# Attention pipelines of a two-block transformer: another step order, probabilities turned a step later, negated minima, and clock fillers

## The chip, the cores and the metric

The kernel runs on one core of a Trainium2 chip. The metric is the device time of one execution in microseconds, median of the runs. One execution was also recorded by the hardware profiler; its rows are what this document reads.

## The reference

Two transformer blocks over 256 tokens of width 1024, in float32. The first block has two layers. Each projects the normed input to twelve groups of columns and runs four attentions with four heads each on them:

```python
a_out = neighbourhood_attention(na_q, na_k, na_v, rel_bias)      # scores + bias, softmax
a = softmax(s1 + alibi) - lam * softmax(s2 + alibi)              # differential attention
b_out = rms_norm(a @ df_v, diff_subln) * (1.0 - lambda_init)
c_out = gqa_attention(rope(rms(gq_q)), rope(rms(gq_k)), gq_v)    # 4 heads, 2 key/value heads
d_out = mla_attention(q_nope, q_rope, k_nope, k_rope, mla_v)
x = x + rms_norm(concat(a_out, b_out, c_out, d_out) @ w_o)       # then a gated FFN
```

`lam` is exp(sum(q1*k1)) - exp(sum(q2*k2)) + lambda_init. The second block has four layers with an FFN each: nsa (compressed, selected and window attention, here 16 causal softmax units of one head), stick-breaking attention, a gated depthwise convolution with layer norm, and moba (8 causal softmax units).

## The kernel before

Five engines run programs of their own, ordered by semaphores that are written out by hand. Weights come in 1 MB pieces into four slots; ScalarE makes a rounded copy `w_hi`, VectorE the rest `w_lo`, and TensorE does three products for each pair (`three`, L2008 to L2010). Activations are split likewise into `hT_hi` and `hT_lo`.

**First block's mixer.** `add_gemm(... (4, 3, 0, 1, 2))` projects the columns in chunks of 512, chunk 4 first, each into two PSUM banks of `acc`, evacuated by ScalarE (token tile 0) and VectorE (tile 1). Between chunks run the latent projections, the rotations (on GpSimd, `gq_rotate` and `ml_rotate`) and the bias flips. In the middle of the last chunk, `jobs_early` turns eight groups of projected tiles (na, gq, mla) into `tiles`. Then `mix_A` runs 20 steps, each two heads (or the two softmaxes of one differential head) of one tile of 128 queries, in `STEP_ORDER`: indices 0 to 3 are neighbourhood steps, 4 to 11 differential, 12 to 15 grouped, 16 to 19 latent. The order is N N N N D D G D D G D D G D D G M M M M.

In turn i of its loop TensorE issues the scores of step i (L2302), turns the probabilities of step i-2 (L2315, into `tr`) and multiplies those of step i-3 with the values (L2335, or L2329 for differential steps). VectorE in turn i takes the negated, scaled minima of step i (L1708 with a bias, L1704 without) and scales the probabilities of step i-1 (L1725, L1726; L1720 to L1722 for differential ones). ScalarE in turn i does the two exponentials of step i (L1254) and the copy of `tr` for step i-2 to `probT` (L1264). Scores lie in two pairs of banks by turns. The differential queries and keys are turned after the scores of step 1 (`diff_jobs`), since their columns come with the last chunk. The exponential for lambda opens ScalarE's `mix_A`. After the last differential step VectorE's `diff_norm` copies the outputs out of `acc`, squares, sums and takes the root in one go, `diff_gain` follows two turns later, and TensorE turns the result at turn 21 (`diff_turn`). Outputs go to `hT_hi` (ScalarE) and `hT_lo` (VectorE) by `pair_out_hi` and `pair_out_lo`. In `pair_steps`, both grouped heads of a step write the same half of the output partitions, and their four products run head after head (`apart` False); in the other steps they alternate between the heads.

**Second block's units.** `unit_pipeline` does the same for nsa and moba, with one head and both query tiles a unit: VectorE adds the bias and takes maxima (L1573), and one more instruction makes `nmx` of them (L1580) before ScalarE's exponentials (L1207). Probabilities are turned (L2242) two units behind the scores (L2227) and multiplied (L2266) three behind, after ScalarE's copy (L1215).

`keep_clock(bank, count)` (L2039) issues products of a constant that nobody reads. Before, it stands only in front of four norms, nine products each.

Of the kernel before, what the change touches and what calls it, by code (L numbers as in the profile page):

```python
# [55 lines left out]
STEP_ORDER = (0, 1, 2, 3, 4, 5, 12, 6, 7, 13, 8, 9, 14, 10, 11, 15, 16, 17, 18, 19)  # L56
NA_LAST, DF_LAST, GQ_LAST = (max(STEP_ORDER.index(i) for i in range(a, b)) for a, b in ((0, 4), (4, 12), (12, 16)))
GQ_FIRST, ML_FIRST = (min(STEP_ORDER.index(i) for i in range(a, a + 4)) for a in (12, 16))
GQ_STEPS = range(12, 16)
JOBS_EARLY, JOBS_A = 8, 10  # L60
EARLY = 4
QUAD = 32
# [145 lines left out]
def make_plan(A):  # L208
# [15 lines left out]
    for index, (kind, l) in enumerate(LAYERS):  # L224
        if kind == "A":
# [3 lines left out]
            def up_projections():  # L229
# [4 lines left out]
            g1 = add_gemm(plan, A["w_in"][l], D, A_IN, "proj", (4, 3, 0, 1, 2), {2: up_projections})  # L234
# [5 lines left out]
                      "lam_ready": 1, "lam_exp": 1, "hT_tr": 1, "kcat_a": 2, "od_ready": 1, "od_taken": 1})  # L240
# [4 lines left out]
            g2.order = (0, 1, 4, 5, 2, 3, 6, 7)  # L245
# [136 lines left out]
def first_second_block(nc, A, out, conv_rows, where_both, where_first, where_second):  # L382
    plan, phases = make_plan(A)
    with ExitStack() as ctx:
# [166 lines left out]
        O_PLACE = {0: 0, 1: 1, 2: 4, 3: 5, 4: 0, 5: 1, 6: 2, 7: 3}  # L551
# [9 lines left out]
        def pair_steps():  # L561
# [3 lines left out]
            def pair(heads, bias=None, scale=1.0, diff=None):  # L565
                for qt in range(TT):
                    steps.append(dict(qt=qt, heads=heads, bias=bias and [b[:, S * qt:S * qt + S] for b in bias],
                                      scale=scale, diff=diff, apart=True))
# [19 lines left out]
            for i in range(GQ_STEPS.start, GQ_STEPS.stop):  # L588
                steps[i]["apart"] = False
# [121 lines left out]
        def jobs_for(kind):  # L711
# [3 lines left out]
            if kind == "A":  # L715
                one = [proj[:, t, col("gq_k"):col("gq_k") + P] for t in range(TT)]
                ks = [[kcat[:, t, 2 * j + i, :] for i in range(2) for t in range(TT)] for j in range(2)]
                return [(two(col("na_q")), tiles[:, 0:2, :], 1.0), (two(col("na_k")), tiles[:, 2:4, :], 1.0),
# [4 lines left out]
                        (two(col("df_q")), tiles[:, 4:6, :], 1.0), (two(col("df_k")), tiles[:, 6:8, :], 1.0)]  # L723
# [114 lines left out]
        def _(pool):  # L838
# [9 lines left out]
            def gq_rotate(ph):  # L848

                pool.wait_ge(sem["gq_root"], n["gq_root"] + 1)  # L850
                for t in range(TT):
# [16 lines left out]
                    def perm(v):  # L868
                        return v[:, 0:4, :].rearrange("p (b a) c -> p a b c", a=2)
                    dst = gq[t][:, 0:4, :].rearrange("p (a b) c -> p a b c", a=2)  # L870
                    link(nc.gpsimd.tensor_tensor(dst, perm(t1), perm(t2), ALU.add))
# [106 lines left out]
        def _(act):  # L978
# [45 lines left out]
            def gemm(ph):  # L1024
                for i, (n0, w, pieces) in enumerate(ph.chunks):
# [12 lines left out]
                    if ph.mix is not None and ph.mix.kind == "mixA" and i == 4:  # L1038
                        for j in range(JOBS_EARLY):
                            _, dst, scale = jobs_for("A")[j]  # L1040
                            evac_job(j, dst, scale, n["pt_ready"])
# [130 lines left out]
            def A_3(ph):  # L1172
                act.wait_ge(sem["lat_a"], n["lat_a"] + 2)
                act.wait_ge(sem["lat_d"], n["lat_d"] + 2)
                for t in range(TT):
                    kv = proj[:, t, A_IN:A_IN + W].rearrange("p (h c) -> p h c", h=ML_H)
                    nc.scalar.activation(kcat[:, t, :, 0:HD], kv[:, :, 0:HD], ACT.Copy).then_inc(sem["kcat_a"], 1)

# [16 lines left out]
            def unit_pipeline(us, jobs, extra={}):  # L1195

                with_T = [i for i, u in enumerate(us) if u["pair"] != 0]
                for i in range(len(us) + 3):
                    if i < len(us):
# [3 lines left out]
                        for qt in range(TT):  # L1203
                            c, cols = 2 * slot + qt, score_columns(u, qt)
                            dst = scores_of(slot)[:, cols]
                            src = dst if u["bias"] is not None else up[:, i % 2, cols]
                            nc.scalar.activation(dst, src, ACT.Exp, bias=nmx[:, c:c + 1],  # L1207
                                                 scale=u["scale"], accum_out=den[:, c:c + 1]).then_inc(sem["p_exp"], 1)
                    if i >= 2 and (i - 2) in with_T:
                        j = with_T.index(i - 2)  # L1210
# [3 lines left out]
                        width = S + P if us[i - 2]["causal"] else TT * S  # L1214
# [9 lines left out]

            def mix_A(ph):
                act.wait_ge(sem["lam_ready"], n["lam_ready"] + 1)
                nc.scalar.activation(lam[:, 0:2], lam[:, 2:4], ACT.Exp).then_inc(sem["lam_exp"], 1)

                def diff_turned():

                    for j in range(JOBS_EARLY, JOBS_A):
                        _, dst, scale = jobs_for("A")[j]
                        if j > JOBS_EARLY:
                            evac_job(j, dst, scale, n["pt_ready"])
                            continue
                        act.wait_ge(sem["pt_ready"], n["pt_ready"] + j + 1)
                        for a in range(2):
                            ins = nc.scalar.activation(dst[:, a, :], tr[:, j % 2, S * a:S * a + S], ACT.Copy,
                                                       scale=c1("df_scale")[:, a:a + 1])
                        ins.then_inc(sem["pt_evac"], 1)  # L1240

# [5 lines left out]
                for i in range(len(steps) + 3):  # L1247
                    if i < len(steps):
                        step, slot = steps[i], i % 4
                        act.wait_ge(sem["s_max"], n["s_max"] + i + 1)  # L1250
                        for u in range(2):
                            c, dst = 2 * slot + u, prob[:, slot, u, :]
                            src = dst if step["bias"] is not None else pair_bank(i, u)
                            nc.scalar.activation(dst, src, ACT.Exp, bias=nmx[:, c:c + 1], scale=-1.0,  # L1254
                                                 accum_out=den[:, c:c + 1]).then_inc(sem["p_exp"], 1)
# [1307 lines left out]
```

## Time and profile before

| | us |
|---|---|
| median of 3 runs | 1963.43 (1956.75 to 1965.12) |
| profiled execution | 1959.28 |
| its span, first to last instruction | 1957.5 |
| TensorE busy | 1867.2 (95%) |
| VectorE busy | 1138.0 (58%) |
| ScalarE busy | 921.6 (47%) |
| GpSimd busy | 175.0 (9%) |
| mean granted TensorE clock | 0.981 |

Busy time of TensorE has modelled ends, so pauses are read from the starts of its instructions, and from the idle time that a row gives in brackets with what ended it. The granted clock of a stretch is 1.00 at 2.4 GHz and 0.50 at 1.2 GHz. L numbers are lines of the kernel above. In the timeline, neighbouring instructions of one kind are merged, with their count behind the x.

### The profile page before, as it was taken

How to read it: one execution, taken by the hardware profiler on the slowest of the kernel's cores; microseconds unless marked ns; L12 is line 12 of the kernel's file. 1: busy time of each engine (PE TensorE's matmuls, PEld its weight loads, DVE VectorE, ACT ScalarE, POOL GpSimd, SP SyncE). 2: the span in 40 equal slices, each digit the busy share in tenths (PEclk: the TensorE clock that was granted, in tenths of full speed). 3: DMA queues.
4: the chain of work that ended last, by engine and by line, in shares of the span. 5: the costliest groups of instructions: out<-in, count | busy, mean ns of one | idle time of the engine just before them, and what ended most of it. 6: DMA issues, size and time to landing. Idle time of an engine off the chain costs nothing. (4 is left out here: it accounts for less than half of the span.)

```text
span 1957.5 us, 29109 instructions
## 1 busy us (share of the span) xinstructions
PE 1867.2 (95%) x11568; PEld 1634.4 (83%) x11568; DVE 1138.0 (58%) x1647; ACT 921.6 (47%) x1267; POOL 175.0 (9%) x213
## 2 busy tenths in 40 slices
PE   7899999988999999899999999999889999989998
PEld 6668999766899978689998789998669998769997
DVE  6676555757655578554446465446765546765443
ACT  4564334456434446554435355345245435564342
POOL 1300000040000030001000001002501002000000
PEclk9999999999999999799999999999989999989999
DMA  7504555550355555126555425554725554524551
GB/s 249 181 22 147 175 183 185 181 172 12 129 193 193 191 187 180 49 87 215 176 204 177 172 86 175 201 182 169 219 90 172 173 202 147 203 91 173 181 204 66
DMA packets 185356, 313.08 MB, mean 160 GB/s; under 512 B 18877, under 2 KB 67571, under 8 KB 185267
## 3 DMA queue, kind: packets, MB, share of 16 engines
q1 hardware_dynamic: 182595, 304.24, 46.0%
q0 software_dynamic: 1376, 4.38, 0.9%
q10 hardware_dynamic: 1296, 3.24, 0.5%
q8 instruction: 60, 0.98, 0.2%
q14 instruction: 29, 0.24, 0.0%
HBM read 309.90 MB, written 1.94 MB: 159 GB/s over the span
## 5 line engine op out<-in xcount | busy, mean ns | idle before, releaser
L1459 DVE TENSOR_TENSOR w_lo<-raw,w_hi 128x2048 fp32r<-128x2048 f32 (+2 forms) x290 | 654.0, 2285 | 289.7 <-ACT w_hi L995 289.0
L995 ACT ACTIVATE w_hi<-raw 128x2048 fp32r<-128x2048 f32 (+2 forms) x290 | 533.5, 1877 | 107.5 <-PE tr L2010 59.8
L2008 PE MATMUL acc<-w_hi,hT_hi 128*128 128x512 f32 (+2 forms) x688 | 270.1, 393 | 13.3 <-DVE w_lo L1459 7.3
L2010 PE MATMUL acc<-w_hi,hT_lo 128*128 128x512 f32 (+2 forms) x688 | 266.4, 387 | 0.0
L2009 PE MATMUL acc<-w_lo,hT_hi 128*128 128x512 f32 (+2 forms) x688 | 266.3, 387 | 0.0
L2008 PE MATMUL acc<-w_hi,aux_hi 128*128 128x512 f32 x608 | 237.2, 390 | 0.0
L2009 PE MATMUL acc<-w_lo,aux_hi 128*128 128x512 f32 x608 | 237.2, 390 | 0.0
L2010 PE MATMUL acc<-w_hi,aux_lo 128*128 128x512 f32 x608 | 236.6, 389 | 0.0
L2008 PE MATMUL up<-hT_hi,w_hi 128*128 128x256 f32 x768 | 217.8, 284 | 0.6 <-DVE w_lo L1459 0.6
L2009 PE MATMUL tr<-hT_lo,w_hi 128*128 128x256 f32 x768 | 217.5, 283 | 0.0
L2008 PE MATMUL tr<-hT_hi,w_hi 128*128 128x256 f32 x768 | 217.5, 283 | 0.0
L2010 PE MATMUL tr<-hT_hi,w_lo 128*128 128x256 f32 x768 | 217.5, 283 | 0.0
L2010 PE MATMUL up<-hT_hi,w_lo 128*128 128x256 f32 x768 | 217.4, 283 | 0.0
L2009 PE MATMUL up<-hT_lo,w_hi 128*128 128x256 f32 x768 | 217.4, 283 | 0.0
L2008 PEld LDWEIGHTS acc<-w_hi,hT_hi 128*128 128x128 f32 x688 | 130.5, 190 | 41.8 <-issue 8.9
L970 POOL TENSOR_TENSOR proj<-proj 128x512 f32<-128x512 f32 x64 | 66.3, 1056 | 1010.9 <-ACT proj L1388 1010.9
L2010 PEld LDWEIGHTS acc<-w_hi,hT_lo 128*128 128x128 f32 x688 | 130.7, 190 | 25.6
L2009 PEld LDWEIGHTS acc<-w_lo,hT_hi 128*128 128x128 f32 x688 | 130.8, 190 | 24.6 <-issue 0.5
L2008 PEld LDWEIGHTS up<-hT_hi,w_hi 128*128 128x128 f32 x768 | 147.3, 192 | 2.7 <-DVE w_lo L1459 1.0
L2009 PEld LDWEIGHTS up<-hT_lo,w_hi 128*128 128x128 f32 x768 | 147.3, 192 | 1.7
L2009 PEld LDWEIGHTS tr<-hT_lo,w_hi 128*128 128x128 f32 x768 | 147.5, 192 | 0.0
L2008 PEld LDWEIGHTS tr<-hT_hi,w_hi 128*128 128x128 f32 x768 | 147.5, 192 | 0.0
(361 smaller groups left out, 2761.1 us busy)
## 6 DMA issues: line engine op xcount, KB each, us to landing
raw<-in_mlp_w_up SPq DMA_DIRECT2D x64, 1024.0 KB, 6.6
raw<-in_mlp_w_down SPq DMA_DIRECT2D x64, 1024.0 KB, 5.4
raw<-in_ffn_w_gate_up SPq DMA_DIRECT2D x88, 512.0 KB, 4.8
raw<-in_ffn_w_down SPq DMA_DIRECT2D x22, 1024.0 KB, 5.1
raw<-in_w_in SPq DMA_DIRECT2D x16, 1024.0 KB, 8.2
raw<-in_sb_w_in SPq DMA_DIRECT2D x12, 1024.0 KB, 5.3
raw<-in_moba_w_in SPq DMA_DIRECT2D x12, 1024.0 KB, 5.3
raw<-in_nsa_w_in SPq DMA_DIRECT2D x10, 1024.0 KB, 6.3
```

Source lines behind the costliest of these rows:

```text
L970: nc.gpsimd.tensor_tensor(ffn_r2[:, W * j:W * j + W], r, r, ALU.mult)\
L995: nc.scalar.activation(w_hi[:, p0.slot, 0:p0.floats], raw[:, p0.slot, 0:p0.floats], ACT.Copy)\
L1459: nc.vector.tensor_tensor(w_lo[:, p0.slot, 0:m], raw[:, p0.slot, 0:m], f32(w_hi[:, p0.slot, 0:m]), ALU.subtract).then_inc(sem["lo_ready"], 1)
L2008: nc.tensor.matmul(dst, hi, whi, start=first, stop=False)
L2009: nc.tensor.matmul(dst, hi, wlo, start=False, stop=False)
L2010: return nc.tensor.matmul(dst, lo, whi, start=False, stop=last)
```

## The change

- The step order becomes D G D G D D G D D G D D N N N N M M M M. The chunks of w_in are taken as 4, 3, 2, 1, 0, so that the neighbourhood's queries and keys come last; `jobs_early` turns the differential tiles (with their two scales) instead, and the na tiles follow after step 4's turn (`late_jobs`).
- Scores, minima and exponentials of the first two steps, and the scaling of the first, are issued within the last chunk. The exponential for lambda moves to the stage before.
- Probabilities are turned three steps behind the scores and multiplied four behind, in both pipelines (`TURN_LAG`, `UNIT_LAG`).
- In grouped steps the second head's output goes to the other half of the partitions, for which GpSimd writes its heads in another order with two more instructions per token tile; all steps alternate between the heads.
- The differential outputs are copied and squared by ScalarE (turn 16); VectorE sums (16), takes the root (17) and applies the gain (18); TensorE turns them at turn 19.
- In the units, minima of negated, scaled scores are taken at once, and L1580 goes.
- Fillers are added: 10 products in moba between the fourth and the fifth turning job, 5 in stick-breaking ahead of the first sums, 16 at the end of the convolution.

```diff
-STEP_ORDER = (0, 1, 2, 3, 4, 5, 12, 6, 7, 13, 8, 9, 14, 10, 11, 15, 16, 17, 18, 19)
+STEP_ORDER = (4, 12, 5, 13, 6, 7, 14, 8, 9, 15, 10, 11, 0, 1, 2, 3, 16, 17, 18, 19)
+TURN_LAG = 3
+STEPS_EARLY = 2
+UNIT_LAG = 3
...
-            g1 = add_gemm(plan, A["w_in"][l], D, A_IN, "proj", (4, 3, 0, 1, 2), {2: up_projections})
+            g1 = add_gemm(plan, A["w_in"][l], D, A_IN, "proj", (4, 3, 2, 1, 0), {2: up_projections})
...
-            g2.order = (0, 1, 4, 5, 2, 3, 6, 7)
+            g2.order = (4, 5, 2, 3, 0, 1, 6, 7)
...
+        def turn_index(j):
+            return JOBS_EARLY + j if j < STEPS_EARLY else JOBS_A + j
-        O_PLACE = {0: 0, 1: 1, 2: 4, 3: 5, 4: 0, 5: 1, 6: 2, 7: 3}
+        O_PLACE = {0: 0, 1: 1, 2: 2, 3: 3, 4: 0, 5: 1, 6: 2, 7: 3}
...
-                pair([head(half_rows(8 + t, HD * u, HD), half_rows(10, HD * u, HD), col("gq_v") + HD * u, HD * t, 4 + u)
-                      for u in range(2)])
+                pair([head(half_rows(8 + t, HD * u, HD), half_rows(10, HD * u, HD), col("gq_v") + HD * u,
+                           HD * (t if u == 0 else 1 - t), 4 + u) for u in range(2)])
...
# GpSimd, gq_rotate
-                    link(nc.gpsimd.tensor_tensor(dst, perm(t1), perm(t2), ALU.add))
+                    link(nc.gpsimd.tensor_tensor(pairs_of[:, :, 0, :], t1[:, 0:2, :], t2[:, 0:2, :], ALU.add))
+                    for head in (2, 3):
+                        link(nc.gpsimd.tensor_tensor(pairs_of[:, 3 - head, 1, :], t1[:, head, :], t2[:, head, :], ALU.add))
...
# ScalarE, gemm, in front of the last chunk's evacuation, behind the early jobs
+                        for j in range(STEPS_EARLY):
+                            pair_exp(pair_steps()[j], j)
# ScalarE, mix_A
+                for i in range(STEPS_EARLY, len(steps) + TURN_LAG + 1):
+                    if i < len(steps):
+                        pair_exp(steps[i], i)
+                    if 0 <= i - TURN_LAG < len(steps):
+                        j = i - TURN_LAG
...
+                    if i == STEPS_EARLY + TURN_LAG - 1:
+                        for j in range(JOBS_EARLY, JOBS_A):
+                            _, dst, scale = jobs_for("A")[j]
+                            evac_job(j + STEPS_EARLY, dst, scale, n["pt_ready"])
...
+                    if i == DF_LAST + 5:
+                        act.wait_ge(sem["o_done"], n["o_done"] + DF_LAST + 1)
+                        nc.scalar.activation(h[:, 0, 0:512], acc[:, 1, :], ACT.Copy).then_inc(sem["od_taken"], 1)
+                        nc.scalar.activation(h[:, 0, 512:1024], acc[:, 1, :], ACT.Square).then_inc(sem["od_taken"], 1)
+                    if i == DF_LAST + 8:
+                        act.wait_ge(sem["hT_tr"], n["hT_tr"] + 1)
+                        pair_out_hi((2, 3))
...
# VectorE, units; the maxima and nmx before
-                        nc.vector.tensor_scalar(nmx[:, c], mx[:, c], -u["scale"], None, ALU.mult)\
-                            .then_inc(sem["s_max"], 1)
+                            ins = nc.vector.tensor_tensor_reduce(
+                                scores_of(slot)[:, cols], up[:, i % 2, cols],
+                                u["bias"][:, cols.start - first:cols.stop - first], -u["scale"], -LOWEST, ALU.add, ALU.min,
+                                nmx[:, c:c + 1])
+                        ins.then_inc(sem["s_max"], 1)
...
# VectorE, mix_A
+                    if i <= len(steps):
+                        pair_scaled(steps[i - 1], i - 1)
+                    if i == GQ_LAST + 6:
+                        pair_out_lo((4, 5), 2)
+                    if i == DF_LAST + 5:
+                        diff_sums()
+                    if i == DF_LAST + 6:
+                        diff_root()
+                    if i == DF_LAST + 7:
+                        diff_gain()
+                    if i == DF_LAST + 8:
+                        pair_out_lo((2, 3), 4)
...
# TensorE, jobs_early
+                pe.wait_ge(sem["evac_a"], n["evac_a"] + 4)
+                pe.wait_ge(sem["evac_d"], n["evac_d"] + 4)
...
+                for i in range(STEPS_EARLY):
+                    pe.wait_ge(sem["pt_evac"], n["pt_evac"] + 2 * (i + 1))
+                    pair_scores(pair_steps()[i], i)
# TensorE, mix_A; diff_turn was at i == 21
+                    if i == STEPS_EARLY + TURN_LAG - 1:
+                        late_jobs()
+                    if i == DF_LAST + 8:
+                        diff_turn()
...
# TensorE, fillers
+                    if j == 4:
+                        pe.wait_ge(sem["evac_a"], n["evac_a"] - 1)
+                        pe.wait_ge(sem["evac_d"], n["evac_d"] - 1)
+                        keep_clock(acc[:, 0, 0:S], 10)
...
+                    if heads[0] == 0:
+                        keep_clock(acc[:, 0, 0:S], 5)
...
+                keep_clock(tr[:, 0, 0:S], 16)
```

## Rows read from the trace of the kernel before

**Rows 1.** The page's costliest groups: count, busy, mean ns, idle before, releaser.

```profile
L2008 PE MATMUL acc<-w_hi,hT_hi 128*128 128x512 f32 (+2 forms) x688 | 270.1, 393 | 13.3 <-DVE w_lo L1459 7.3
```

**Rows 2.** Stage windows: length, busy of five engines, clock, DMA share, GB/s.

```profile
84.70:132.90 48.20, 41.14 (x285) 28.19 (x284) 38.42 (x146) 32.85 (x111) 0.00 (x0) 0.93 0.01 1
125.80:132.70 6.90, 5.87 (x34) 4.25 (x36) 3.85 (x11) 3.80 (x11) 0.00 (x0) 0.51 0.01 2
430.20:481.10 50.90, 42.49 (x286) 28.97 (x285) 38.40 (x146) 34.25 (x112) 0.00 (x0) 0.90 0.01 1
803.70:845.80 42.10, 39.27 (x208) 29.42 (x208) 28.54 (x155) 26.97 (x92) 0.00 (x0) 0.94 0.00 1
1131.40:1136.70 5.30, 5.29 (x33) 5.30 (x34) 2.83 (x6) 3.24 (x8) 0.00 (x0) 0.68 0.00 0
1436.00:1443.40 7.40, 0.19 (x1) 0.00 (x0) 6.87 (x19) 2.78 (x8) 0.00 (x0) 0.77 0.00 1
1443.40:1447.10 3.70, 3.62 (x9) 2.94 (x10) 2.17 (x6) 3.70 (x11) 0.00 (x0) 0.54 0.00 0
1720.00:1725.10 5.10, 0.12 (x2) 0.00 (x0) 4.93 (x6) 0.75 (x2) 0.00 (x0) 0.82 1.00 354
1725.10:1733.50 8.40, 7.69 (x28) 5.94 (x28) 1.68 (x11) 4.67 (x10) 0.00 (x0) 0.50 0.06 21
154.80:158.90 4.10, 4.05 (x19) 3.23 (x17) 2.76 (x12) 0.69 (x2) 0.00 (x0) 1.00 0.45 178
```

**Rows 3.** Groups by line and shape, whole span.

```profile
L1254 ACT ACTIVATE prob<-prob,small 128x256 f32<-128x256 f32 x48 | 23.9, 500 | 10.6 <-DVE small L1708 10.5
...
L1722 DVE SCALAR_TENSOR_TENSOR prob<-prob,small 128x256 f32<-128x256 f32 x16 | 7.7, 484 | 1.7
...
L1725 DVE TENSOR_SCALAR prob<-prob,small 128x256 f32<-128x256 f32 x24 | 8.5, 354 | 0.9
...
L1264 ACT ACTIVATE probT<-tr 128x512 f32<-128x512 f32 x24 | 14.0, 585 | 2.3 <-PE tr L2315 2.3
```

**Rows 4.** Timeline, layer 0: start, length, engine, line, operation, tiles, count, idle.

```profile
92.24 0.70 PE L2302 MATMUL up<-tiles 32*128 32x256 f32 x4
...
92.99 0.42 DVE L1708 CUSTOM_DVE_ANT_0 prob<-up,region 128x256 f32<-128x256 f32 x1 [0.43 <-PE up L2302]
...
95.42 0.66 PE L2335 MATMUL acc<-probT,proj 128*64 128x128 f32 x8
...
96.01 0.70 PE L2302 MATMUL up<-tiles 64*128 64x256 f32 x4
...
97.86 0.70 PE L2302 MATMUL acc<-tiles 32*128 32x256 f32 x4
```

**Rows 5.** Timeline, layer 0: a grouped heads' output and the next scores.

```profile
103.03 1.06 PE L2335 MATMUL acc<-probT,proj 128*64 128x128 f32 x8 [0.25 <-DVE hT_lo L1695]
...
104.01 0.70 PE L2302 MATMUL up<-tiles 32*128 32x256 f32 x4
```

**Rows 6.** Timeline, tail of layer 0's attention.

```profile
123.71 0.17 DVE L1472 TENSOR_SCALAR small<-small 128x8 f32<-128x8 f32 x1
...
125.53 0.69 DVE L1704 TENSOR_REDUCE small<-acc 128x2 f32<-128x512 f32 x1
...
126.83 1.09 PE L2315 MATMUL tr<-both,prob 128*128 128x128 f32 x4 [3.11 <-DVE prob L1725]
```

**Rows 7.** Timeline, starts of the attention stages, layers 0 and 1.

```profile
89.71 0.66 PE L2315 MATMUL tr<-both,prob 128*128 128x128 f32 x4 [2.12 <-ACT tiles L1238]
...
431.05 1.28 ACT L1227 ACT_TABLE_LOAD   x1
```

**Rows 8.** Timeline, one unit of nsa.

```profile
822.81 0.17 DVE L1580 TENSOR_SCALAR small<-small 128x2 f32<-128x2 f32 x1
```

**Rows 9.** Waits, whole span: total us, times, longest.

```profile
PEld tr L2242 <- DVE prob L1600: 8.1, 12, 1.3
```

**Rows 10.** Timeline, stick-breaking, TensorE's first sums.

```profile
1131.40 0.46 PE L2413 MATMUL tr<-prob,region 128*128 128x128 f32 x2 [2.35 <-DVE prob L1871]
```

More of the change, by code:

```diff
@@ L1223, in mix_out_hi, with pair_exp @@
                     nc.scalar.activation(hT_hi[:, k, :], accT[:, k, :], ACT.Copy).then_inc(sem["hT_hi"], 1)
[L1225 to L1240 removed]
+            def pair_exp(step, i):
+                slot = i % 4
+                act.wait_ge(sem["s_max"], n["s_max"] + i + 1)
+                for u in range(2):
+                    c, dst = 2 * slot + u, prob[:, slot, u, :]
+                    src = dst if step["bias"] is not None else pair_bank(i, u)
+                    nc.scalar.activation(dst, src, ACT.Exp, bias=nmx[:, c:c + 1], scale=-1.0,
+                                         accum_out=den[:, c:c + 1]).then_inc(sem["p_exp"], 1)
+            def mix_A(ph):
                 def pair_out_hi(ks):
@@ L1517, in gemm @@
                         turned_lo(ph.then, range(KT // 2))
+                    if ph.mix is not None and ph.mix.kind == "mixA" and i == 4:
+                        steps_early(ph.mix.l)
                     dve.wait_ge(sem["piece_used"], pieces[-1][0] + 1)
@@ new lines, in steps_early, with pair_max @@
+                for i in range(STEPS_EARLY):
+                    pair_max(steps[i], i)
+                    if i:
+                        pair_scaled(steps[i - 1], i - 1)
+            def pair_max(step, i):
+                slot = i % 4
+                dve.wait_ge(sem["s_ready"], n["s_ready"] + i + 1)
+                if step["bias"] is None:
+                    nc.vector.tensor_reduce(nmx[:, 2 * slot:2 * slot + 2], pair_banks(i), AX_X, ALU.min)\
+                        .then_inc(sem["s_max"], 1)
+                else:
+                    for u in range(2):
+                        ins = nc.vector.tensor_tensor_reduce(
+                            prob[:, slot, u, :], pair_bank(i, u), step["bias"][u], -step["scale"], -LOWEST, ALU.add,
+                            ALU.min, nmx[:, 2 * slot + u:2 * slot + u + 1])
+                    ins.then_inc(sem["s_max"], 1)
@@ new lines, in pair_scaled @@
+            def pair_scaled(step, i):
+                slot = i % 4
+                c = slice(2 * slot, 2 * slot + 2)
+                dve.wait_ge(sem["p_exp"], n["p_exp"] + 2 * (i + 1))
+                link(nc.vector.reciprocal(rec[:, c], den[:, c]))
+                p0, p1 = prob[:, slot, 0, :], prob[:, slot, 1, :]
+                r0, r1 = (rec[:, 2 * slot + u:2 * slot + u + 1] for u in range(2))
+                if step["diff"] is not None:
+                    mark(nc.vector.tensor_scalar(r1, r1, lam[:, 4:5], None, ALU.mult))
+                    link(nc.vector.tensor_scalar(p0, p0, r0, None, ALU.mult))
+                    nc.vector.scalar_tensor_tensor(out=p1, in0=p1, scalar=r1, in1=p0, op0=ALU.mult, op1=ALU.add)\
+                        .then_inc(sem["p_norm"], 2)
+                else:
+                    nc.vector.tensor_scalar(p0, p0, r0, None, ALU.mult).then_inc(sem["p_norm"], 1)
+                    nc.vector.tensor_scalar(p1, p1, r1, None, ALU.mult).then_inc(sem["p_norm"], 1)
@@ L2105, in jobs_early, with pair_scores @@
                     job(j, jobs_for("A")[j][0], n["pt_evac"])
+                for i in range(STEPS_EARLY):
+                    pe.wait_ge(sem["pt_evac"], n["pt_evac"] + 2 * (i + 1))
+                    pair_scores(pair_steps()[i], i)
+            def pair_scores(step, i):
+                for u, head in enumerate(step["heads"]):
+                    last = nc.tensor.matmul(pair_bank(i, u), head["q"][:, P * step["qt"]:P * step["qt"] + P], head["k"],
+                                            start=True, stop=True)
+                last.then_inc(sem["s_ready"], 1)
             def lag_turn():
```

232 lines of the change are left out of this document (78 added, 154 removed).

## The prediction, as it stood before the result was known

> **What bounds the kernel now.** I read the page's costliest groups first: TensorE runs the split matmuls almost without a pause (13.3 us idle before the largest group, in 270 us of it) [rows 1]. So time is to be had only where TensorE waits or runs at its lower clock. Next the stage windows [rows 2]: in the attention stages of the first block (48.2 and 50.9 us) and in the nsa mixer (42.1 us) the granted clock is 0.93, 0.90 and 0.94, and DMA is idle (0.01). Three short stretches are lower still: 0.68 in stick-breaking, 0.77 then 0.54 around the convolution's end, 0.82 then 0.50 in moba. Then the order of time inside a stage [rows 4 to 7] and the waits [rows 9]. The profiled execution took 1959.28 us (span 1957.5); the median shown is 1963.43, 4.15 more. The sum is made against the first and carried to the second.
>
> **Attention of the first block: the ring.** TensorE's turn i holds scores S(i), turned probabilities T, and output product O. From 92.24 to 96.01 two turns take 3.77 us, 1.885 each [rows 4]: 0.75 from the start of S until VectorE begins, two minima begun 0.35 apart, two exponentials of 0.50, behind them in ScalarE's order the probT copy of 0.585 [rows 3], then O, 0.59 from 95.42 to 96.01. The new lag shifts T, copy and O together by a turn: O(i-4) still waits for the copy that ScalarE makes behind exp(i-1). The ring keeps its 1.88. What gains slack is only VectorE's scaling ahead of T.
>
> *Pairing.* The grouped heads' O takes 0.98 (103.03 to 104.01) against 0.59, as both heads write the same 64 partitions [rows 4, 5]. The new placement alternates the halves: 0.4 less, 8 times, 3.2 us at most; below, nothing, where the ring waits for the copy anyway. In the middle O is a link of the ring, so I take nearly all of it, inside the 1.88. The Trainium skill, TensorEngine Tiling (Array Packing), PSUM Bottleneck, says that tiling speeds up TensorE but not the copies out of PSUM; by it these 3.2 us would be lost and the sum below would be 10.4 instead of 13.6. The trace agrees only by half: the copy is in the ring, but so is O.
>
> *Start.* The first two S, minima and exponentials go into the last w_in chunk. There TensorE pays them (2 x 0.53 = 1.06), while VectorE and ScalarE were idle until the chunk's end. The lambda exponential goes too; in layer 1 it cost a table load of 1.28 on ScalarE with everything behind it [rows 7]. The 2.12 us that TensorE waited before T(0) go [rows 7]. What is late next: the two moved transpose jobs now wait for the copies of T(0) and T(1), and these stand behind exp(3) and exp(4). From the chunk's end E: evacuation and minima of step 2 until 1.7; exp(2) to 2.7; minima(3) by 3.2, exp(3) and a 0.38 copy to 4.6; VectorE's differential scaling (0.16 + 0.13 + 0.35 + 0.48, about 1.2 with links) and minima(4) by 5.05; exp(4) and copy(1) to 6.7; second job to 7.3; O(0), S(5), T(2), O(1), S(6), T(3) to 10.3; O(2) behind copy(2), at 11.1. Step 7's S then starts at E + 11.1. Before, it started at 97.86 [rows 4], 13.1 after the chunk, with one more T and O done (about 0.9), so 12.2 against 11.1 + 1.06: nothing gained in layer 0.
>
> *Middle.* Steps 7 to 15 at 1.88: 17.0 us.
>
> *Tail.* Before, VectorE did the differential norm at one place: a root of nine dependent instructions (123.71 to 125.53) ahead of the last minima (125.53), TensorE stood 3.11 us, and the rest ran at clock 0.51 to 132.91 [rows 2, 6]. Now copy and squares go to ScalarE at turn 16, sum, root and gain to VectorE at turns 16, 17, 18, the transpose to TensorE's turn 19. But each engine works in order. From S(16) = 0: minima 1.9; exp, copy and the two new ScalarE passes (0.59 each) to 4.7; VectorE's sum waits for these, to 5.4, and minima(17) behind it to 6.1; scaling 6.9; root 8.75; minima(18) 9.4; scaling 10.3; gain (two 0.7 passes) 11.75; TensorE's transpose waits for that and ends at 12.3. Then O(15) and T, O of four more steps with 1.2 us of waits: 18.2. So one stall of 3.1 becomes two near 1.9 (before O(14), before the transpose).
>
> Sum: 1.06 + 11.1 + 17.0 + 18.2 = 47.4 us per layer. Against 48.2 and 50.9 that is 0.8 and 3.5, together **4.3**. Bounds: by TensorE's issue alone S 13.8, T 8.5, O 11.0, jobs and turn 1.6 make 35; with 4 of fill 39, so 21 gained at most. With the tail at half clock as before (T and O near 1.05, not 0.53 and 0.59) 50.5: 2 lost. I take 4.3.
>
> The added GpSimd adds (two more per token tile, about 0.5 us each) lie in a stage where GpSimd ends some 6 us before its consumer; without that cover 1 to 2 us a layer. The new waits of the early jobs (chunk 4 of 5 evacuated) are met long before; behind them stands only TensorE itself. The reversed chunks only deliver na_q and na_k last: nothing. w_o starts with pieces split beforehand; its third and fourth are split by ScalarE behind the mixer, as before.
>
> **Units of nsa and moba.** Their ring is of the same kind. The small nmx instruction goes out of it: 0.17 and its link, about 0.21 between VectorE and ScalarE [rows 8], once in two turns: 0.21 x 8 = 1.7 us for the 16 units of nsa, 0.8 for the 8 of moba. The third turn of lag takes away TensorE's waits for scaling ahead of T, 8.1 us in 12 places of the two mixers together [rows 9], 5.4 and 2.7 by units. But T's wait and O's wait for the copy stand in one queue, and what the first gives the second mostly takes, as the ring goes on at its pace; so I count a good eighth, 0.7 and 0.5, between nothing and all. Nsa: **2.4** (0.5 to 7), moba's units 1.3 (0 to 3.5). The half clock in which nsa's units start (0.94 over the stage [rows 2]) is touched by no edit.
>
> **Clock fillers.** A filler of 9 products is 18 instructions and 4.05 us at full clock, and over such a stretch the clock reads 1.00 [rows 2] (the window from 154.80): 0.45 a product. Moba: 10 products, 4.5 us, in a pause of 5.1 with 0.12 us of TensorE work. They end before the next jobs. What goes is the 0.50 window from 1725.1, 8.4 us with 7.7 of TensorE: four jobs and the first three S. Without it half of the issue time would go, 3.8; the evacuations between jobs and the first minima and exponentials, which don't depend on this clock, keep some 1.4 of that: 2.4. With the units' 1.3, **3.7** for moba (0 to 7). Conv: 16 products, 7.25 us, in a pause of 7.4 (1436.0 to 1443.4); the gemm behind it ran 3.3 of the next 3.7 us at half clock (0.54 in the mean): **1.6** (0 to 1.7). Stick-breaking: 5 products, 2.3 us, in 2.35 of idle time [rows 10]; 5.3 us of sums at 0.68 would take 3.6: **1.6** (0 to 1.7), as ScalarE's weights and its next table load move up with it.
>
> **Sum.** 4.3 + 2.4 + 3.7 + 1.6 + 1.6 = 13.6. 1959.28 - 13.6 = 1945.7; for the median 1963.43 - 13.6 = **1949.8**. The stages behind are bound by TensorE, so nothing gives this back.
>
> **Rivals.** (a) Tails stay slow: the two stalls of 1.9 bring the half clock in each attention tail, 3 us a layer, and the copies swallow the pairing. The two stages then give -2 for 4.3, the sum is 7.3, 1956.1. For it: two shorter pauses at layer 1's start were followed by a low clock (0.90 over the stage). Against: in layer 0 a like start kept the full clock. (b) The lag decouples more: if ScalarE and VectorE run ahead so that O never waits for the copy, the attention stages come half way to TensorE's 39, 12 us instead of 4.3, the sum is 21.3: 1942.1. Against: the ring has no slack that the lag adds. (c) The other side: a filler meets the half clock. If TensorE is at 1.2 GHz when the fillers begin, they take double: 9.1 in a pause of 5.1, 14.5 in 7.4, 4.5 in 2.35, which is 4.0 + 7.1 + 2.2 = 13.3 lost, and their gain (1.6 + 1.6 + 2.4) is gone: 8.0 saved elsewhere less 13.3 is 5.3 slower, 1968.7. It decides from the point where the fillers of moba and conv are both caught (11.1 and 4.0 of gain, against 13.6). Against: all three places had full clock when the pause began (0.77 and 0.82 are the means with the fall inside). (d) The copies out of PSUM hold the grouped turns at their old length though O is 0.4 shorter: 3.2 less, sum 10.4, 1953.0. For it: the copy is a link of the same ring [rows 3, 4]. Against: O follows it and is not beside it. This is the rule cited under pairing. (e) The early steps not hidden (VectorE's evacuation late): 2 us a layer less, inside the range.
>
> **Chances.** Forecast with its own range 1945 to 1953: 0.45. (a) 0.2, (b) 0.18, (c) 0.05, (d) 0.07, (e) 0.05. Range for 8 in 10: 1938 to 1959, which takes in (b), (d), (e) and most of (a), not (c). About 0.5% (9.8 us, so 1953.6) is what a measurement tells from no change. Faster: forecast, (b), and most of (d): 0.67. Same: (a), (e), a rest: 0.28. Slower: 0.05.
>
> **What would show it.** Right: attention stages near 47 us each, no 3.1 us wait before the last T, but VectorE waiting about 2 us for ScalarE's square at turn 16 and TensorE waiting near 1.9 before the differential transpose; grouped O at 0.59; periods of 1.88 in the middle. The moba stretch and the gemm behind conv at clock 1.00, fillers ending within 0.5 us of what they wait for. nsa's stage near 39.7 us with scaling absent from T's releasers. Wrong: periods under 1.8 (b), half clock in the tails (a), fillers at 0.45 an instruction (c).

## The result and the profile after

The changed kernel takes 1969.84 us (median of 10 runs, 1966.94 to 1973.97) against 1963.67 of the kernel before on the same chip: ratio 1.0043, 95% interval 1.003 to 1.0055. I had forecast 1949.8 and a range up to 1959. The profiled execution has a span of 1968.5 (before 1957.5) and a mean granted clock of 0.972 (before 0.981), the first sign of where to look.

I split both executions at the first split product behind each mixer. Length of a stage here is from the last split product ahead of the mixer to the first behind it, starts of instructions. Stage lengths, here and below, are of the one profiled execution of each kernel:

| stage | before | after | difference | change of the lead or lag, row to row |
|---|---|---|---|---|
| attention, layer 0 | 48.48 | 56.81 | +8.3 | +10.2 |
| attention, layer 1 | 51.18 | 57.31 | +6.1 | +7.5 |
| nsa | 62.66 | 61.57 | -1.1 | +0.15 |
| stick-breaking | 25.81 | 24.27 | -1.5 | -1.55 |
| convolution | 45.67 | 43.58 | -2.1 | -3.6 |
| moba and the end | 31.22 | 28.70 | -2.5 | -1.7 |

The last column says by how much the changed kernel falls behind (+) or catches up (-) from one row's end to the next, so it also holds the products between the stages, and it adds up to +11.0. A row ends at the first split product behind its mixer; the convolution's goes on to moba's mixer, over products that ran at half clock before, and moba's to the end of the program. Both attention rows hold the stretch of early jobs inside the last chunk of w_in, 1.68 us longer with the two scores that moved there (5.20 to 6.87 in layer 0). By stage lengths four of six rows are gains; with what lies in front of them, the two attention rows lose 17.7 us.

The windows of the changed kernel, which answer to [rows 2] (length, busy time of TensorE, weight load, VectorE, ScalarE, GpSimd, granted clock, DMA share, GB/s): the two attention stages whole, the half clock in each, the nsa mixer, the convolution's filler and the products behind it, and moba.

```profile
86.30:143.10 56.80, 50.85 (x279) 34.09 (x277) 34.80 (x134) 31.86 (x103) 0.00 (x0) 0.67 0.00 1
90.90:118.20 27.30, 26.29 (x114) 17.48 (x114) 14.77 (x63) 14.04 (x47) 0.00 (x0) 0.50 0.00 1
441.50:498.80 57.30, 50.33 (x279) 33.66 (x277) 34.88 (x134) 31.75 (x103) 0.00 (x0) 0.70 0.00 1
449.30:483.50 34.20, 34.20 (x151) 22.57 (x151) 20.10 (x83) 17.57 (x63) 0.00 (x0) 0.50 0.00 1
821.60:863.70 42.10, 38.59 (x209) 30.71 (x209) 26.29 (x139) 27.04 (x92) 0.00 (x0) 0.92 0.00 1
1450.30:1457.70 7.40, 7.03 (x33) 5.86 (x32) 6.93 (x19) 2.77 (x7) 0.00 (x0) 1.00 0.00 0
1457.70:1461.40 3.70, 3.68 (x16) 3.10 (x17) 2.16 (x6) 3.70 (x11) 0.00 (x0) 1.00 0.00 0
1738.80:1747.00 8.20, 6.18 (x35) 4.19 (x34) 4.47 (x26) 6.75 (x20) 0.00 (x0) 1.00 0.02 6
```

The clock over an attention stage is 0.67 and 0.70, where it was 0.93 and 0.90. It reads 0.50 for 27.3 us in layer 0 and 34.2 us in layer 1, and in the second of these TensorE is busy 34.20 of 34.20: no pause is left in it, and yet it stays at 1.2 GHz. Behind the convolution and in moba the fillers did what they were for: 1.00 in place of 0.54 and 0.50.

Where the half clock of layer 0 begins, TensorE's timeline (start, length, operation, in brackets the idle time before it and what ended it):

```profile
88.85 0.66 PE L2324 MATMUL tr<-both,prob 128*128 128x128 f32 x4
90.93 1.08 PE L2150 MATMUL tr<-both,proj 128*128 128x128 f32 x4 [1.42 <-ACT probT L1262]
92.99 1.12 PE L2150 MATMUL tr<-both,proj 128*128 128x128 f32 x4 [0.97 <-ACT probT L1262]
93.90 0.96 PE L2342 MATMUL acc<-proj,probT 128*128 128x64 f32 x4
94.78 1.22 PE L2127 MATMUL acc<-tiles 32*128 32x256 f32 x4
...
96.56 1.12 PE L2347 MATMUL acc<-probT,proj 128*64 128x128 f32 x8
97.61 1.23 PE L2127 MATMUL up<-tiles 64*128 64x256 f32 x4
```

The two late transpose jobs wait for the copies of T(0) and T(1), as my start said. The clock reads half from 90.94 on, so in this layer it fell at the end of the first pause, before the second. From there the first job's four transposes take 1.08 where those of T just before took 0.66, scores 1.22 and a grouped output product 1.12, where they take 0.70 and 0.66 at full clock in the start-filled kernel below. A turn from 94.78 to 97.61 takes 2.83 us, where the ring had 1.885 [rows 4]. From start to start the pauses are 1.70 and 1.39 here, 1.69 and 1.70 in layer 1, where the half clock begins at 449.3, just behind the second job's start (448.19). When it ended does not go with the kind of step: in layer 0 at 118.2, with transposes and outputs of differential and grouped steps still running behind the first two neighbourhood scores (which have the grouped ones' shape), in layer 1 at 483.5, behind all four neighbourhood scores and the first of a latent step:

```profile
117.14 1.23 PE L2127 MATMUL acc<-tiles 64*128 64x256 f32 x4
118.67 0.66 PE L2347 MATMUL acc<-probT,proj 128*64 128x128 f32 x8
...
479.56 2.02 PE L2127 MATMUL up<-tiles 96*128 96x256 f32 x4
```

Layer 0 has a second fall, in its tail: half clock from 131.9 to 142.1.

### The profile page after: what moved, and what is told of

Read it like the earlier page. It is cut to its first block and busy times, and to the rows that moved or that the text cites. A ratio compares the mean times of both kernels' runs of the same rounds, so it can differ in the third digit from the quotient of the medians.

```text
span 1968.5 us, 29217 instructions
## 1 busy us (share of the span) xinstructions
PE 1891.4 (96%) x11630; PEld 1652.6 (84%) x11630; DVE 1132.4 (58%) x1619; ACT 924.3 (47%) x1271; POOL 176.6 (9%) x221
## 5 line engine op out<-in xcount | busy, mean ns | idle before, releaser
L2021 PEld LDWEIGHTS acc<-w_lo,hT_hi 128*128 128x128 f32 x688 | 130.7, 190 | 24.6 <-issue 0.5
```

Source lines behind the costliest of these rows:

```text
L2021: nc.tensor.matmul(dst, hi, wlo, start=False, stop=False)
```

## Experiments

The changed kernel is "after", the one with fillers in the start pauses "start-filled"; stages are measured as above. Each ratio is against the kernel before, run beside it.

**1. Fill the pauses.** In `late_jobs`, three products of ones ahead of each job:

```
                     for j in range(JOBS_EARLY, JOBS_A):
+                        keep_clock(acc[:, 0, 0:S], 3)
                         job(j + STEPS_EARLY, jobs_for("A")[j][0], n["pt_evac"])
```

> The changed kernel (1969.8) with three products of ones put ahead of each of the two late transpose jobs of the attention stages (where TensorE stands 1.70 and 1.39 us in layer 0, 1.69 and 1.70 in layer 1), six a layer, nothing else. Theory 1 (these pauses begin the half clock, and the turns behind them are slow because of the clock alone): granted clock 1.00 from 91 us on in place of half clock until 118.25, and from 449 in place of half until 483.5; some ten turns a layer at 1.9 in place of 2.5 to 2.95 us, so 8 to 10 us less a layer: 1950 to 1955. Theory 2 (the third step of lag or the new order makes the turns slow, the clock only reads low): turns stay at 2.5 us, 1970 within 2.

Measured: 1950.62, ratio 0.994 (0.9923 to 0.9958). Theory 1. The filled start, then three windows: layer 0 behind the start, its tail, and layer 1 whole.

```profile
88.65 0.66 PE L2325 MATMUL tr<-both,prob 128*128 128x128 f32 x4
89.14 1.46 PE L2054 MATMUL acc<-both 128*128 128x256 f32 x6
...
92.78 0.66 PE L2150 MATMUL tr<-both,proj 128*128 128x128 f32 x4 [0.19 <-ACT probT L1262]
...
91.00:118.00 27.00, 25.63 (x183) 16.81 (x181) 20.36 (x88) 21.07 (x71) 0.00 (x0) 1.00 0.00 1
122.30:132.60 10.30, 9.28 (x47) 6.24 (x45) 5.92 (x17) 5.31 (x16) 0.00 (x0) 0.50 0.01 2
432.30:478.40 46.10, 39.74 (x291) 26.35 (x289) 34.34 (x134) 31.61 (x103) 0.00 (x0) 1.00 0.01 1
```

The jobs start where they did (92.78 for 92.99, stage start 0.2 earlier); in the same 27 us TensorE issues 183 instructions in place of 114. The stages are 47.90 and 46.05 long, 8.9 and 11.3 less. Between these two the only difference is the tail at half clock in the first: 1.85 us for 10.2 us of it. In all seven kernels here with fillers in both start pauses (this one and those of experiments 3, 4, 5, 7 and 8) none of the 14 profiled starts is followed by a fall; of the six starts of this order without fillers (the changed kernel, experiment 2, the first kernel of experiment 3) five are.

**2. Does the work itself keep the clock down?** One product of ones ahead of the scores of turns 5 to 13, the pauses left as they were:

```
+                        if 5 <= i < 14:
+                            keep_clock(pair_bank(i, 0), 1)
                         pair_scores(step, i)
```

> The changed kernel with one product of ones (0.45 us at full, 0.9 at half clock) ahead of the scores of turns 5 to 13 of the attention stages: nine a layer, in the middle of the half clock. If the turns of differential and grouped heads are what keeps the clock low once it has fallen (their scores use 32 or 64 rows and their products 64 columns), the fuller product brings it back before 118 and 483 us: some 5 turns a layer at 0.9 less against 9 fillers of 0.45 to 0.9, so 1966 to 1972 with the half clock shorter by 8 us or more a layer. If the clock comes back when it does for a reason that has nothing to do with what TensorE does, the half stretches keep their 27 and 34 us and the kernel is 8 to 16 us longer: 1978 to 1986. The pauses in front (1.70, 1.39) stay in both.

Measured: 1962.84, ratio 1.0007 (0.9994 to 1.002), stages 53.49 and 53.36. The first branch, with a time 3 us under its range. Windows of the half clock behind the start and of the stretch after it, layer 0 (layer 1 has the same two lengths):

```profile
94.40:101.30 6.90, 6.90 (x28) 3.65 (x27) 2.53 (x10) 1.72 (x6) 0.00 (x0) 0.51 0.00 0
101.30:128.60 27.30, 25.21 (x178) 16.82 (x177) 21.08 (x89) 18.86 (x64) 0.00 (x0) 1.00 0.00 1
```

The clock falls as before and is back after 6.9 us in place of 27.3 and 34.2. So two things made the loss: the pauses begin it, and the turns by themselves, though issued without a pause, left it standing for 27.3 and 34.2 us; with one full product more a turn it ended after 6.9, in both layers. That differential and grouped turns are to blame, as my expectation had it, is not shown: in layer 1 of the changed kernel the four neighbourhood scores (468.46 to 476.75) ran at half clock as well.

**3. The third step of lag.** `TURN_LAG = 2` in the changed kernel, and then in the start-filled one, where the clock is not in the way:

> The changed kernel with the attention stages' probabilities turned two steps behind the scores, as before, instead of three; the units of nsa and moba keep three. If the third step is what costs in the attention stages (17.7 us in the two), they come back to within 3 us of before: 1955 or less. If the half clock begun by the late jobs is what costs, it depends on where the late jobs (now one turn earlier) wait: they stand behind two copies still, so the pauses stay, the clock is half for 25 us or more again, and the time is within 4 of 1970.

> The same kernel (start fillers) with the attention stages' probabilities turned two steps behind. By my prediction the third step is worth nothing in the ring (its period is set by exponentials, copy and O): stages within 1 of 47.90 and 46.05, if the clock stays up; 1949 to 1952. If the third step is what decouples the engines (rival b), the stages get 2 us or more longer each: 1955 or more. With two steps T waits for VectorE's scaling, so I look for more than 2 us of such waits in the stage; and for full clock from the start on, as the fillers stand in the late jobs here too.

Measured: 1965.18, ratio 1.0003 (0.9981 to 1.0025), and 1959.56, ratio 0.9987 (0.9975 to 0.9998). The first time fits neither branch, and it is a lesson of its own: its pauses ahead of the second late job are the same in both layers, and the clock fell in layer 0 only (stages 60.80 and 49.92). Its ten runs go from 1955.73 to 1970.95, at mean clocks from 0.987 to 0.976. The job and the window behind it, layer 0 and then layer 1:

```profile
91.48 0.95 PE L2150 MATMUL tr<-both,proj 128*128 128x128 f32 x4 [0.75 <-ACT probT L1262]
...
91.70:119.00 27.30, 27.30 (x124) 17.90 (x122) 15.11 (x63) 13.55 (x47) 0.00 (x0) 0.50 0.00 1
...
450.69 0.66 PE L2150 MATMUL tr<-both,proj 128*128 128x128 f32 x4 [0.76 <-ACT probT L1262]
...
447.50:474.00 26.50, 22.20 (x162) 14.11 (x160) 22.12 (x96) 20.82 (x72) 0.00 (x0) 1.00 0.01 2
```

In the start-filled pair the stages are 51.04 and 51.05 for 47.90 and 46.05, so 3.1 and 5.0 longer with two steps. Not all of it is the lag. With two steps the late jobs wait less than the fillers in front of them last: from the chunk's end to S(5) takes 8.48 with fillers and 7.35 without (layer 1 of the kernel above), 1.1 lost to the fillers. The tail's clock takes a part too (6.8 us of half clock in layer 1, by experiment 1 about 1.2). An estimate of the third step's worth is then 2.0 and 2.7. T waits 2.6 and 3.2 us for VectorE's scaling, as looked for. So the second branch's number, but not its mechanism: from S(5) to S(15) the ring takes 18.21 with two steps of lag and 18.25 with three. The loss is in the tails (TensorE's timeline of layer 1 with two steps):

```profile
463.73 0.66 PE L2348 MATMUL acc<-probT,proj 128*64 128x128 f32 x8 [1.78 <-DVE hT_lo L1727]
...
470.74 0.63 PE L2325 MATMUL tr<-both,prob 128*128 128x128 f32 x4 [1.12 <-DVE prob L1701]
...
475.39 0.66 PE L2304 MATMUL acc<-both,h 128*128 128x128 f32 x4 [0.87 <-DVE h L1720]
478.96 1.12 PE L2348 MATMUL acc<-probT,proj 128*64 128x128 f32 x8 [2.91 <-DVE hT_lo L1727]
```

Outputs of latent steps go where the turned differential outputs lie, and outputs of neighbourhood steps where the grouped ones lie, so they wait for VectorE's `hT_lo`; a turn earlier they wait 1.78 and 2.91 for it.

**4. Pairing.** Undone in the start-filled kernel, and done alone in the kernel before:

```
+            for i in range(12, 16):
+                steps[i]["apart"] = False
```

> The changed kernel with the start fillers (1950.6, attention stages 47.90 and 46.05 at full clock but for the first one's tail), and in it the pairing of the grouped heads undone: both heads of a step write the same 64 partitions again. My term for the pairing was 3.2 for the two layers, 1.6 a layer: if output products are a link of the ring, the stages become 1.6 longer each, 1953.8. By rival (d) (the copies out hold the turn) nothing changes: 1950.6 within 1. If the column-halved products are also what lets the clock go, the half clock would be shorter in the first tail here, which I do not expect.

> The kernel before with the pairing of the grouped heads alone. In the changed kernel it was worth 1.45 us a layer with tails alike (49.35 against 47.90). If it is a link of the old ring too, the two attention stages go from 48.48 and 51.18 by 1.45 each: 1960.5 against 1963.5, clock falls of 2 us either way. By rival (d) no difference: 1963.5.

Measured: 1955.01, ratio 0.9962 (0.9943 to 0.998), stages 49.35 and 49.35, both with a tail at half clock, against 47.90 with such a tail: 1.45 a layer, near the 1.6 of the first branch, and not rival (d)'s nothing. The tails' half clock is as long as with pairing (10.2), so the halved products are not what lets the clock go there. A grouped output product, unpaired and paired (its first start to the next scores 1.02 and 0.58):

```profile
98.87 1.09 PE L2351 MATMUL acc<-probT,proj 128*64 128x128 f32 x8 [0.36 <-ACT probT L1264]
...
98.66 0.66 PE L2348 MATMUL acc<-probT,proj 128*64 128x128 f32 x8 [0.27 <-ACT probT L1262]
```

In the kernel before it gave 1961.84, ratio 0.9999 (0.9975 to 1.0023): not seen in the time (1962.94 for the kernel before beside it), since layer 1's stage came out at 53.99 with the clock at half for 13.7 us at its start and 6.8 in its tail. By the scores' starts in layer 0, at full clock, the stretch from 99.51 to 121.56 (22.05) became 20.92, 1.1 less.

**5. Units of nsa and moba.** `UNIT_LAG = 2` in the start-filled kernel, with the output work a turn earlier:

> The same kernel (start fillers) with the units of nsa and moba turned two steps behind the scores as before the change; the negated minima stay. My terms: the third step is worth 0.7 in nsa and 0.5 in moba, the minima 1.7 and 0.8. The trace of the changed kernel has a new wait of 3.13 (nsa) and 1.63 (moba) ahead of the first output product. If the third step only buys that wait, nsa and moba get 1 to 3 us shorter without it: stages 60.53 and 28.71 to 58.5 and 27.7, 1947 to 1949. If the lag is worth what I gave it: 1.2 longer, 1951.8.

Measured: 1948.91, ratio 0.9933 (0.9913 to 0.9953). nsa 60.47 (60.53 with three), moba 28.30 (28.71). The third step is worth nothing in nsa and costs 0.4 in moba. The wait that it makes in nsa, in the changed kernel, and the same place with two steps:

```profile
827.35 0.55 PE L2263 MATMUL tr<-both,prob 128*128 128x128 f32 x3
830.75 0.92 PE L2285 MATMUL acc<-probT,proj 128*128 128x256 f32 x4 [2.86 <-ACT probT L1227]
...
807.34 0.55 PE L2263 MATMUL tr<-both,prob 128*128 128x128 f32 x3 [0.20 <-DVE prob L1594]
807.87 0.92 PE L2285 MATMUL acc<-probT,proj 128*128 128x256 f32 x4
```

**6. The three fillers alone**, in the kernel before:

> The kernel before with the three clock fillers of the change alone (10 products in moba, 16 behind the convolution's sums, 5 ahead of stick-breaking's sums). My prediction's terms are 2.4, 1.6 and 1.6: 5.6 less, 1958. The changed kernel's stages gave 3.6 behind the convolution and 1.6 in stick-breaking: with 2.4 in moba 7.6 less, 1956. If the fillers take PE's time where it isn't idle (rival c), 1964 or more.

Measured: 1954.96, ratio 0.9972 (0.9943 to 1.0002). Stick-breaking 24.28 (1.5 less), moba's stage 29.06 (2.2 less), the convolution 42.09. Against experiment 5 this prices the minima: nsa 62.76 to 60.47 and moba 29.06 to 28.30, 2.3 and 0.8. Of the 2.3, some 0.5 is the clock: the half clock of 27.3 us around nsa's start begins 1.7 us ahead of the stage here and 2.8 ahead of it in experiment 5, so 1.1 us less of it lies inside, at half speed. By that estimate the minima are worth about 1.8 in nsa. The time itself is not clear of noise, as the interval takes in 1.

**7. How much filling it takes.** One product a pause in place of three:

> The changed kernel with one product in each of the two start pauses in place of three (so 1.2 and 0.9 to 1.2 us of pause are left of 1.7 and 1.4). If the length of the idle stretch decides (the lag-two variant kept the clock over pauses of 0.83 and about 1), the clock may hold: 1951 to 1953. If the two pauses together with the thin work between them decide, one product isn't enough, and the half clock of 27 us is there in one or both layers: 1960 to 1970. By my theory 1 both can be; it only says that the time follows the clock, 9 us a layer in which it falls.

Measured: 1948.18, ratio 0.9932 (0.9909 to 0.9955), stages 46.07 and 46.06. The pauses that are left did not lower the clock in the profiled execution (mean clock 0.991). In the other five runs the mean clock is 0.987 to 0.991. By estimate, a mean lower by 0.004 is 15 us more of half clock over the whole run, less than one fall of 27:

```profile
90.86 0.66 PE L2150 MATMUL tr<-both,proj 128*128 128x128 f32 x4 [0.90 <-ACT probT L1262]
93.00 0.66 PE L2150 MATMUL tr<-both,proj 128*128 128x128 f32 x4 [1.06 <-ACT probT L1262]
```

**8. More fillers, and a version that beats both.** Three products ahead of O(14), three ahead of the differential transpose, four ahead of O(16); in nsa three ahead of the second compressed product, nine between the transpose jobs, five ahead of the compressed values' transpose:

> The same kernel (start fillers) with more of them: in the attention tail 3 ahead of the output product of step 14, 3 ahead of the differential transpose and 4 ahead of the output product of step 16 (pauses of 1.9, 1.1 to 1.8 and 2.0); in nsa 3 ahead of the second compressed product (pause 1.43), 9 between the query jobs (4.18) and 5 ahead of the compressed values' transpose (2.39). Theory 1: full clock from 91 us to the end of the first layer's tail (1.85 less, as the two layers' stages differ by that) and in nsa from 777 to 805 us, where 13 us of TensorE work are done at half clock: 4 to 6 less. 1943 to 1945. If nsa's half clock comes from something else than the pauses ahead (the small 30-row products), nsa keeps its 60.5 us or pays for fillers at half clock, 5 us: 1949 to 1954.

Measured: 1945.78, ratio 0.9913 (0.9893 to 0.9933): attention 46.08 and 46.06, nsa 56.99 for 60.53. The gain in nsa came, a little under what I expected. That in attention is not shown to be these fillers' work: the kernel of experiment 5, without them, kept the clock through both tails too (46.08 and 46.07), and in experiment 7 a tail with 3.4 us of half clock still gave 46.06. With start fillers alone the tail's clock falls in some executions and not in others; in the two kernels with tail fillers it fell in none of the four tails. With two steps of unit lag and two products more in nsa:

> All that helped, together: start fillers, tail and nsa fillers (1945.8), the units turned two steps behind (0.4 less in moba, 0.1 in nsa), and two more products in nsa while TensorE waits 1.11 us for the last copies ahead of the units, where the clock is half from 795 to 802 us. Sum of the measured parts 1945.3; if the two products bring the clock back 3 us earlier, 1 less: 1944.3. Range 1943 to 1946. If the fillers' gains don't add (a clock that falls at another place), 1947 to 1949.

Measured: **1944.18**, ratio 0.9906 (0.9881 to 0.9931), nsa 56.52, moba 28.26. It is 18.8 us under the kernel before and 25.7 under the changed one. Windows of the two attention stages and of nsa's stage; 10.2 us at half clock are left around nsa's start, 6.7 of them inside the stage:

```profile
88.10:134.20 46.10, 44.05 (x311) 29.81 (x309) 34.35 (x134) 31.64 (x103) 0.00 (x0) 1.00 0.01 1
432.70:478.70 46.00, 43.96 (x310) 29.77 (x308) 34.34 (x134) 31.64 (x103) 0.00 (x0) 1.00 0.00 1
781.70:838.20 56.50, 53.64 (x301) 43.34 (x301) 34.19 (x153) 35.28 (x113) 0.00 (x0) 0.94 0.12 40
```

## Why the prediction was wrong

- **The step that failed** is "Start" of the attention stage, with its rival (a). I worked out both waits of the late jobs to tenths of a us (second job at E + 7.3) and priced them as time only. I judged the clock by one look backwards, "in layer 0 a like start kept the full clock", and looked for its fall in the tails, at 3 us a layer. It fell at the start, and stayed down for 27.3 and 34.2 us. Price: 56.81 - 46.07 and 57.31 - 46.06, 10.7 and 11.3 us, 22 together (experiments 1, 7, 8). Of layer 0's, 1.85 is its tail at half clock, so rival (a) came true in one of the two tails, at less than its 3 us. The trace of before had the warning, and rival (a) names it, but carries it to the tails alone. TensorE's timeline at the start of its layer 1:

```profile
431.30 1.09 PE L2126 MATMUL tr<-both,proj 128*128 128x128 f32 x8
433.79 0.70 PE L2302 MATMUL up<-tiles 64*128 64x256 f32 x4 [1.40 <-DVE small L1708]
436.61 1.12 PE L2315 MATMUL tr<-both,prob 128*128 128x128 f32 x4 [2.12 <-ACT tiles L1238]
```

Two pauses in a row (1.67 and 2.50 from start to start), and the clock at half from 436.4 on, for 3.4 us. Layer 0, which I took for the like case, had only the second of them [rows 7]. But one pause can be enough: in experiment 6 that start of layer 0 is unchanged, and the clock fell behind its one pause, for 3.4 us, as it did in the second kernel of experiment 4:

```profile
91.97 0.76 PE L2315 MATMUL tr<-both,prob 128*128 128x128 f32 x4 [2.12 <-ACT tiles L1238]
92.66 1.23 PE L2302 MATMUL acc<-tiles 64*128 64x256 f32 x4
```

So what I had was one execution of a start that goes either way. Why the low clock lasts 3.4 us in one place and 34 in another is open. The order of the steps doesn't settle it: with neighbourhood turns in front it lasted 3.4 us in these three places and 13.7 in layer 1 of experiment 4's second kernel.

- **The ring and the sum of the stage were right.** At full clock, in the kernel with more fillers of experiment 8, E to S(7) takes 11.3 (11.1 predicted), S(7) to S(16) 16.5 (17.0), S(16) to the end 18.3 (18.2), the rows below. The early scores made the last chunk 1.68 longer for my 1.06, so the sum is 47.8 for 47.4. Against 48.48 and 51.18 that is 0.7 and 3.4: most of my 4.3 us would have been there. The two stalls that I had placed are there, before O(14) and the differential transpose, and a third, ahead of O(16) for `hT_lo`, which I had only within my "1.2 us of waits"; the last three rows show them without fillers, in layer 1 of experiment 1. The last product of the chunk in the kernel with more fillers, the scores of steps 7 and 16, and the three waits:

```profile
88.00 0.39 PE L2022 MATMUL acc<-w_hi,hT_lo 128*128 128x512 f32 x1
...
99.26 0.70 PE L2127 MATMUL acc<-tiles 32*128 32x256 f32 x4
...
115.78 1.08 PE L2127 MATMUL up<-tiles 96*128 96x256 f32 x4
...
467.43 0.66 PE L2348 MATMUL acc<-probT,proj 128*64 128x128 f32 x8 [1.61 <-ACT probT L1262]
471.09 0.66 PE L2304 MATMUL acc<-both,h 128*128 128x128 f32 x4 [1.50 <-DVE h L1720]
474.66 0.66 PE L2348 MATMUL acc<-probT,proj 128*64 128x128 f32 x8 [1.73 <-DVE hT_lo L1727]
```

- **Lag in the attention stages**: no gain in the ring, as said. That it carries the tail over the differential norm and the shared output places (an estimate of 2 to 3 us a layer, experiment 3) was in my tail's sum, without my seeing that the lag was what paid for it. Rival (b)'s price was also added up wrong: half way from 48.2 and 50.9 to 39 is 10.6 us, not 12.
- **Pairing**: 1.45 a layer for 1.6. Rival (d), by which the copies hold the grouped turns at their old length, is ruled out by it: the product is a link of the ring as much as the copy.
- **Units**: the minima gave 2.3 (about 1.8 at like clock) and 0.8 for my 1.7 and 0.8; the third step 0 and -0.4 for my 0.7 and 0.5: its copy stands behind one exponential more at the start, and the first output product waits for it. nsa's stage gained 1.1 and not 2.4, and the products ahead of it took 1.2 longer. The second is the clock: the 27.3 us of half clock began 4.6 us ahead of the stage in place of 2.0, and 2.6 us at half speed are 1.3 lost, by estimate. Inside the stage a second fall of 3.4 us made up for that, 26.1 us of half clock for 25.4 before (0.92 for 0.94 over the mixer).
- **Fillers**: stick-breaking 1.5 for 1.6, moba 2.2 for 2.4. The convolution gave 3.6 for 1.6; 1.4 of that is a fall at 1419.5 of before that did not come in this execution of after. In executions with it on both sides (experiment 1) it is 2.2. Rival (c), fillers caught at half clock, did not happen there; in experiment 8 the nine fillers of nsa were for their first 1.4 us, and nsa still gained.
- **The sum**: 13.6 forecast, 11.0 lost, 24.6 apart: 22 the clock of the attention stages, 2.6 nsa, 2.0 moba (its end reads half clock for 3.6 in place of 2.1 us), less 2.0 in the convolution.

The Trainium skill, TensorE: Matmul & The Clock Gate (HAM clock gate), states that activity releases the throttle and that idleness brings it back. The trace agrees with each half only in part. Pauses of 1.70 and 1.39 us, once filled, no longer brought the half clock, but in nsa it also came with TensorE busy throughout (last section). And TensorE was busy 34.20 of 34.20 us while the clock stayed at 0.50; with one full product more a turn it was back after 6.9 us.

## What to carry to other kernels

Price a pause of TensorE twice: its own length, and the work behind it at half clock, for as long as nearby stretches of the same kind of work have shown it to last. Here two pauses of 1.4 to 1.7 us cost 9 to 11 us a layer, and one filler product in each, which finds TensorE idle anyway, bought that back. One execution in which a pause left the clock alone is no evidence that the next one will. Read the clock of stretches before judging an edit: the runs of the kernel before go up and down with it (1953.61 at a mean clock of 0.983, 1967.71 at 0.977, on one chip), so compare stage lengths at equal clock, and look where a fall begins, too: part of it may lie outside the stage.

## What the runs showed of the hardware

- A low clock can outlast the pause by 27 and 34 us with TensorE never idle (27.30 busy of 27.30 in layer 0 of experiment 3, 34.20 of 34.20 in layer 1 of the changed kernel); 6.9 us when one 128x256 product a turn is added.
- The same pauses (0.75 and 0.76 us idle in experiment 3) may or may not lower it: in one layer they did, in the other not.
- In nsa the clock falls in each of the 13 profiled kernels, also where no pause is left ahead of it. With the pause filled, TensorE is busy throughout, first with 30-row products and then with a gemm of few columns, and reads 0.51 from 778.1 on (the kernel with more fillers):

```profile
768.70:774.60 5.90, 5.90 (x98) 5.80 (x97) 5.36 (x7) 2.48 (x5) 0.00 (x0) 1.00 0.80 285
774.60:778.10 3.50, 3.50 (x36) 3.50 (x33) 3.33 (x7) 2.70 (x2) 0.00 (x0) 1.00 1.05 391
778.10:785.00 6.90, 6.90 (x31) 6.63 (x31) 5.62 (x10) 1.41 (x6) 0.00 (x0) 0.51 0.76 248
```

So a pause is not the only thing that lowers it. What in this work does was not taken apart.
